# A conditioning sum in two rounded products, and the key tile of the mixing stages in three

## The reference, cut to what matters

```python
for l in range(DEPTH):                      # DEPTH = 2
    x = layer_norm(ALPHA * x + swiglu_half(x, ffn1_w1[l], ffn1_w3[l], ffn1_w2[l]), ...)
    h = x @ w_in[l]                         # 1024 -> 3360 columns
    (a_u, a_v, b_qkv, b_z, b_beta, b_decay, c_q, c_k, c_v, c_r, c_g) = split(h)
    out_b = gated_deltanet(b_qkv, ...)      # conv of 4 taps, silu, q and k normalized per head
    ...
    x = layer_norm(ALPHA * x + concatenate([out_a, out_b, out_c]) @ w_out[l], ...)
    x = layer_norm(ALPHA * x + swiglu_half(x, ffn2_w1[l], ffn2_w3[l], ffn2_w2[l]), ...)
```

## Time and profile before

| | |
|---|---|
| median of 3 runs | 2219.01 us (2215.41 to 2221.36) |
| the profiled execution | 2216.92 us, of which 2215.1 us are the span |
| TensorE busy | 97% of the span |
| VectorE busy | 46% |
| ScalarE busy | 33% |
| GpSimd busy | 4% |
| granted TensorE clock | 1.00 of full speed |
| HBM traffic | 632.39 MB, mean 285 GB/s |

### The profile page before, as it was taken

One profiled execution on the slowest core, in us unless ns is written; L12 is line 12 of the kernel. 1 busy time (PEld: TensorE's weight loads), 2 busy tenths in 40 slices (PEclk: granted clock), 3 DMA queues, 4 the chain that ended last, 5 costly groups with the idle time before them and its releaser, 6 DMA issues. The chain is left out here.

```text
span 2215.1 us, 30365 instructions
## 1 busy us (share of the span) xinstructions
PE 2153.3 (97%) x12435; PEld 1330.2 (60%) x12436; DVE 1025.1 (46%) x1419; ACT 728.0 (33%) x1134; POOL 91.5 (4%) x139
## 2 busy tenths in 40 slices
PE   8999999999999999999999999999999999999998
PEld 7887877888888787788877643333333333333332
DVE  5664776855766568676559741111111111111111
ACT  5433334533543343363436631111111111111111
POOL 5000020000000002000011000000000000000000
PEclk9999999999999999999999999999999999999999
DMA  9762422786487352178636679999999999999998
GB/s 329 232 237 89 156 77 86 246 288 217 134 282 245 120 179 82 41 234 270 218 129 192 261 308 418 429 428 428 428 429 428 429 428 428 428 428 428 428 428 350
DMA packets 192741, 632.39 MB, mean 285 GB/s; under 512 B 31296, under 2 KB 127568, under 8 KB 166272
## 3 DMA queue, kind: packets, MB, share of 16 engines
q1 hardware_dynamic: 192640, 630.93, 73.7%
HBM read 629.82 MB, written 1.07 MB: 285 GB/s over the span
## 5 line engine op out<-in xcount | busy, mean ns | idle before, releaser
L450 PE MATMUL banks<-room_rounded 128*128 128x512 f32 x1824 | 430.4, 391 | 0.0
L450 PEld LDWEIGHTS banks<-room_rounded 128*128 128x128 f32 x1824 | 339.5, 188 | 69.0
L390 DVE TENSOR_TENSOR room_rounded<-memory,room_rounded 128x2048 fp32r<-128x2048 f32 x132 | 299.3, 2292 | 101.4 <-ACT room_rounded L384 96.2
L3351 DVE TENSOR_SCALAR attend_words<-banks 128x512 f32<-128x512 f32 x32 | 22.1, 692 | 557.0 <-PE banks L3087 557.0
L384 ACT CAST room_rounded<-memory 128x2048 fp32r<-128x2048 f32 x132 | 247.8, 1904 | 72.4 <-PE banks L468 63.5
L468 PE MATMUL banks<-room_rounded 128*128 128x512 f32 x1056 | 248.2, 390 | 0.3
L3087 PE MATMUL banks<-memory 128*64 128x512 f32 x1088 | 242.7, 594 | 0.0
L468 PEld LDWEIGHTS banks<-room_rounded 128*128 128x128 f32 x1056 | 197.6, 188 | 42.8 <-DVE room_rounded L637 2.1
L3087 PEld LDWEIGHTS banks<-memory 128*64 128x64 f32 x1088 | 75.1, 136 | 150.8 <-issue 147.7
L3087 PE MATMUL banks<-attend_later,memory 128*64 128x512 f32 x672 | 152.1, 594 | 0.1
L547 ACT ACTIVATE memory<-banks 128x256 f32<-128x256 f32 x88 | 33.8, 384 | 313.0 <-PE banks L450 295.4
(11 more groups left out here) (473 smaller groups left out, 2756.2 us busy)
## 6 DMA issues: line engine op xcount, KB each, us to landing
memory<-in_ffn_w SPq DMA_DIRECT2D x132, 1024.0 KB, 7.4
memory<-in_w_gate_up SPq DMA_DIRECT2D x62, 2048.0 KB, 22.5
attend_later<-in_w_gate_up SPq DMA_DIRECT2D x39, 2048.0 KB, 23.8
memory<-in_w_down SPq DMA_DIRECT2D x25, 2048.0 KB, 24.1
attend_later<-in_w_down SPq DMA_DIRECT2D x19, 2048.0 KB, 23.4
attend_words<-in_w_gate_up SPq DMA_DIRECT2D x17, 2048.0 KB, 22.7
memory<-in_w_in SPq DMA_DIRECT2D x32, 1024.0 KB, 7.1
memory<-in_w_ada SPq DMA_DIRECT2D x32, 768.0 KB, 5.3
```

The costliest lines, as they stand in the source:

```text
L390: nc.vector.tensor_tensor(b, chip.ring[:, chip.slot(base + i), :], a.bitcast(F32), ALU.subtract).then_inc(chip.used, 1)
L450: m = nc.tensor.matmul(psum[:, GU + tt, :], x_parts[:, xp, k, tt * P:tt * P + P], rows, start=(n == 0), stop=(n == 3 * KD - 1))
L3351: ts(room.gate, psum[:, GATE_BANK, :], 7.0, None, ALU.min).then_inc(s["g_ready"], 1)
```

## The change: what it does

Two things are changed. `sum_ada` takes its operand in two rounded parts, so six rounded products stand for three plain ones; ScalarE makes the leading part (`ada_lead`) in the last step of the stage, and VectorE the rest (`ada_low`) ahead of the sums of the norm. In the mixing stages the key tile is in parts as well: two casts on ScalarE ahead of `evac(3)`, two subtractions on VectorE ahead of `finish_x`, and three rounded products on TensorE. To make room for the new leading parts buffers move (`last_lead`, `late`, `x_low`, `lg_rows`). The queries and keys are no longer copied out of PSUM by VectorE: ScalarE squares them from there, `back(1)` goes to banks 2 and 3, and VectorE multiplies by the inverse norms straight from PSUM.

```diff
@@ sum_ada
-        pe.wait_ge(chip.used, base + load_ada(ADA_ROWS - 1) + 1)
+        pe.wait_ge(*s.at("ada_low", 1))
         for i in range(3):
-            nc.tensor.matmul(psum[0:3, MOD_BANK, :], chip.pick[:, 2 - i:5 - i], ada_acc[:, i * 512:i * 512 + 512],
-                             start=(i == 0), stop=(i == 2))
+            for part in (ada_lead, chip.ada_low):
+                nc.tensor.matmul(psum[0:3, MOD_BANK, :], chip.pick[:, 2 - i:5 - i], part[:, i * 512:i * 512 + 512],
+                                 start=(i == 0 and part is ada_lead), stop=(i == 2 and part is chip.ada_low))
@@ ffn_phase, scalar
                 silu(ft, 1)
+                if ft + 1 == STEPS:
+                    act.wait_ge(chip.used, base + load_ada(ADA_ROWS - 1) + 1)
+                    nc.scalar.copy(ada_lead, ada_acc).then_inc(s["ada_lead"], 1)
@@ ffn_phase, vector
+            dve.wait_ge(*s.at("ada_lead", 1))
+            tt_op(chip.ada_low, ada_acc, ada_lead.bitcast(F32), ALU.subtract).then_inc(s["ada_low"], 1)
             norm.sums(dve, 0)
@@ mix_phase
-IN_PARTS = (1, 2)
+IN_PARTS = (1, 2, 3)
...
-                pe.wait_ge(s["low"], 3 + half if t == IN_PARTS[0] else SPLITS)
+                pe.wait_ge(s["low"], 3 + half if t == IN_PARTS[0] else NT + 2 * (t - IN_PARTS[0] + 1))
@@ mix_phase, tensor
-            back(1, 4)
+            back(1, 2)
@@ mix_phase, scalar
             lead(act, 2, 1)
-            for n in range(1, 4):
-                evac(n)
+            evac(1)
+            evac(2)
+            lead(act, 3, 0)
+            lead(act, 3, 1)
+            evac(3)
...
             silu(1)
+            for t, bank in ((0, 4), (1, 2)):
+                for tt in range(NT):
+                    act.wait_ge(s["back"], 2 * t + tt + 1)
+                    func(sq[:, tt, 512 * t:512 * t + 512], psum[:, bank + tt, :], ACT.Square).then_inc(s["squared"], 1)
@@ mix_phase, vector
             take_mod(chip, s)
-            for i in range(2):
-                low(dve, IN_PARTS[1], i, 5 + i)
+            for i in range(4):
+                low(dve, IN_PARTS[1 + i // 2], i % 2, 5 + i)
             finish_x(chip, s, dve, chain)
...
-            take_back(0, 4)
             convolve(1, range(4))
...
-            take_back(1, 4)
-
-            dve.wait_ge(s["tok"], 4)
-            chain(tt_op(sq, qk, qk, ALU.mult))
-            nc.vector.tensor_reduce(ss.rearrange("p (t h) -> p t h", t=NT), sq, AX, ALU.add).then_inc(s["ss"], 1)
+            dve.wait_ge(s["squared"], 2 * NT)
+            nc.vector.tensor_reduce(ss.rearrange("p (t h) -> p t h", t=NT), sq.rearrange("p t (h d) -> p t h d", d=64), AX, ALU.add)\
+                .then_inc(s["ss"], 1)
...
-                chain(tt_op(qk[:, tt, :, :], qk[:, tt, :, :], each_col(rn[:, 16 * tt:16 * tt + 16], 64), ALU.mult))
+                for i, bank in enumerate((4, 2)):
+                    chain(tt_op(qk[:, tt, 8 * i:8 * i + 8, :], heads(bank + tt),
+                                each_col(rn[:, 16 * tt + 8 * i:16 * tt + 8 * i + 8], 64), ALU.mult))
                 scale_first(tt)
```

More of the change, by code:

```diff
@@ L113, in __init__ @@
         self.gbT = w.take(16).rearrange("p (s k) -> p s k", s=2)
-        self.pick = w.take(5)
+        self.pick = self.rounded[:, w.at:w.at + 5]
+        w.take(5)
         self.modT = w.take(24).rearrange("p (s k) -> p s k", s=3)
@@ L119, in __init__ @@
         self.bias_table = self.rounded[:, w.at + D:w.at + 2 * D]
+        odd = w.at % 8
+        self.ada_low = nc.alloc_sbuf_tensor_at("ada_low", [P, ADA_BLOCK + odd], F32R, offset=at + 4 * (w.at - odd))[:, odd:odd + ADA_BLOCK]
         self.norm_gb = w.take(2 * D).rearrange("p (s d) -> p s d", s=2)
@@ L651, in ffn_phase @@
     return Stage(norm, lead, low, emit)
-FFN = "columns acc_zero acc_bias mod_row mod_stored pchain gu0 gu1 x_lead x_low lead hidden hidden_lead hidden_low turned gate down chain " + POST_NORM
+FFN = "columns acc_zero acc_bias ada_lead ada_low mod_row mod_stored pchain gu0 gu1 x_lead x_low lead hidden hidden_lead hidden_low turned gate down chain " + POST_NORM
 def ffn_counts(NT, steps, rows_before, mod_before):
     tiles = sum(what != "ada" for what, *_ in ffn_order(steps))
-    counts = dict(acc_zero=1, acc_bias=16, gu0=steps, gu1=steps, x_lead=NT, x_low=NT, lead=tiles, hidden=NT * steps, hidden_lead=steps,
+    counts = dict(acc_zero=1, acc_bias=16, ada_lead=1, ada_low=1, gu0=steps, gu1=steps, x_lead=NT, x_low=NT, lead=tiles, hidden=NT * steps, hidden_lead=steps,
                   hidden_low=steps, turned=steps, gate=NT * steps, down=steps - 1 + 2 * NT, norm_gbT=32, variance=NT, deviation=NT,
@@ L775, in _ @@
                 nc.gpsimd.memset(chip.eps[:, i:i + 1], v)
-            chain(nc.gpsimd.memset(chip.pick, 0.0))
-            nc.gpsimd.memset(chip.pick[:, 2:3], 1.0)
+            chain(nc.gpsimd.memset(chip.pick.bitcast(F32), 0.0))
+            nc.gpsimd.memset(chip.pick[:, 2:3].bitcast(F32), 1.0)
         @block.sync
@@ L840 @@
        "ub_mm wt_mm ub wt scan_a scan_q u_rows scan_o o_rows scan_s state b_ss b_rms b_out "
-       "mixed_turned mixed_T mixed lead low ") + POST_NORM
+       "mixed_turned mixed_T mixed lead low squared ") + POST_NORM
 def mix_loads(chip, l, w_in, w_out):
@@ L872, in mix_phase @@
     LT, PT = (per_head(region[:, 1024 * i:1024 * i + 1024]) for i in range(2))
-    x_low = rounded("low", w.at, 2048)
     x_first = rounded("x_first", w.at + 2048, 2048)
-    first_leads = rounded("first_leads", w.at + 4096, 8 * MT)
+    x_low = rounded("low", w.at + 4096, 2048)
+    first_leads = rounded("first_leads", w.at + 6144, 8 * MT)
     out_first = rounded("out_first", w.at - 1060, 2048)
@@ L884, in mix_phase @@
     dm = per_head(dm)
-    late = rounded("late", w.at + 1024, 4096)
     out_later = rounded("out_later", w.at, 6144)
@@ L893, in mix_phase @@
     U = per_head(turned_k)
+    late = rounded("late", w.at, 4096)
     levels = w.take(2048)
@@ L901, in mix_phase @@
     WT = scaled_q.rearrange("p (t c g n) -> p t c g n", t=NT, c=2, g=4)
+    last_lead = rounded("last_lead", w.at, 2048)
     qdT = w.take(1024).rearrange("p (t g n) -> p t g n", t=NT, g=4)
@@ L909, in mix_phase @@
     SCt = take3(4, 64)
-    lg_rows = per_head(chip.tmp.rearrange("p t d -> p (t d)")[:, 0:1024])
+    lg_rows = bk
     sgw, sgT = take3(4, P), take3(4, P)
@@ L925, in mix_phase @@
     x_parts = (by_k(x_first), by_k(x_low))
-    lead_rooms = (first_leads[:, 0:4 * MT], first_leads[:, 4 * MT:8 * MT], late[:, 0:2048], late[:, 2048:4096])
+    lead_rooms = (first_leads[:, 0:4 * MT], first_leads[:, 4 * MT:8 * MT], late[:, 0:2048], late[:, 2048:4096],
+                  chip.tmp_rounded, last_lead)
     def tile_parts(t, i):
@@ L946, in mix_phase @@
     end = base + NW + 4
+    sq = chip.tmp
     heads = lambda bank: psum[:, bank, :].rearrange("p (h n) -> p h n", h=8)
@@ L1078, in back @@
                 pe.wait_ge(s["silu"], t + 1)
+                if t == 0:
+                    pe.wait_ge(s["par"], 1)
+                elif t == 1:
+                    pe.wait_ge(s["dm_arg"], 2)
                 for tt in range(NT):
-                    n = 2 * t + tt
-                    if n == 0:
-                        pe.wait_ge(s["par"], 1)
-                    if n >= 2:
-                        pe.wait_ge(s["tok"], n - 1)
                     for c in range(4):
@@ L1161, in turn_heads @@
             def turn_heads(tt):
[L1163 removed]
                 if tt == 0:
[L1165 to L1166 removed]
+                    pe.wait_ge(s["scaled"], 2)
                 else:
@@ L1380, in _ @@
             solution(1)
-            pe.wait_ge(s["tok"], 6)
+            pe.wait_ge(s["tok"], 2)
             scan(0, lambda: unit(12, 0, 4), lambda: unit(12, 4, 8))
@@ L1819, in _ @@
                     take_back(2, 0)
-                    dve.wait_ge(s["tok"], 6)
+                    dve.wait_ge(s["tok"], 2)
                     scale_values(0)
```

5 lines of the change are left out of this document (1 added, 4 removed).

## The result

| | before | after |
|---|---|---|
| median, us | 2217.69 (20 runs beside those of after) | 2222.92 (20 runs, 2218.62 to 2228.57) |
| ratio to before, 95% | | 1.0023 [1.0015, 1.0031] |
| profiled execution: time; span; granted clock | 2216.92; 2215.1; 1.00 | 2221.38; 2219.6; 0.995 |

The change costs 5.2 us (2222.92 - 2217.69): inside the 0.3% called no change, but the 95% interval lies wholly above 1. The predicted time was 2222.3, in a range from 2214 to 2228; the predicted change was +3.3.

A forecast was written before the change was run, and what follows sets the result against it. Ahead of the experts TensorE is hardly ever idle, so shifts there were taken to reach the end whole. First mixing stage +4.7, second +2.5, feed-forward ends -3.9 make +3.3 us on the median 2219.01: 2222.3, range 2214 to 2228.

The forecast's parts named there:

- The conditioning sum, -3.9: Feed-forward ends: six rounded products for three plain ones free 1.3 us at three ends, 0 at the fourth.
- The covers: Feed-forward ends: ScalarE's 1.43 us cast fits a 2.78 us wait, VectorE's 1.72 us subtraction a 1.73 us wait; cost 0.
- the rival on the norm's sums: Feed-forward ends: VectorE's subtraction pushes the norm's sums, up to 6.9 us over four ends, 2229.2; chance 0.06.
- The stands: Mixing stages: TensorE waits at gate_low and for glowT behind key tile splitting; 6.2 us late in the first, 4.0 second.
- The rounded unit, 1.3 each: Key tile on TensorE: a unit in parts takes 5.9 us against 7.20, two units in each mixing stage.
- unit 6 saving nothing: First mixing stage: the decay gates' chain, also 6.2 us late, sets the time, so only unit 7 saves 1.3.
- the loads come in time: Rival, mixing stages: key tile lands early enough, both stages gain 5.6 us together, kernel 9.5, to 2209.5; chance 0.12.
- Queries and keys, -0.2: Mixing stages: TensorE's 1.53 us wait ahead of back(1) shortens by 0 to 1.5 us, taken as 0.2.
- The clock: Rival, mixing stages: granted clock falls in the new 4.1 us stand, making the kernel slower; chance 0.12.
- I am wrong if [...] the granted clock leaves 1.00 there: Sign against the forecast: casts end before TensorE reaches gate_low, or granted clock leaves 1.00 there.
- Behind that TensorE does not wait for VectorE until the level products, so the rest is worth 0: Mixing stages, behind the wait ahead of back(1): VectorE's remaining freed time gains 0.
- 4.7 + 2.5 - 3.9 = +3.3: Sum in us: first mixing stage 6.2 - 1.3 - 0.2, second 4.0 - 1.3 - 0.2, feed-forward ends -3.9.

The follow-up runs named there:

- sum_only: The kernel before with only the conditioning sum in rounded parts; 0.9979 of the kernel before.
- no_sum: The changed kernel with the conditioning sum back in three plain products; 1.0044 of the kernel before.
- late_split: The changed kernel with the key tile's casts moved behind the silu and fifth evac, its subtractions behind glowT; 0.9978 of the kernel before.
- late_rest: The changed kernel with only VectorE's two key tile subtractions moved behind the copy glowT; 1.0015 of the kernel before.
- early_loads: The changed kernel with the key tile's two loads issued earlier on SyncE, engine orders kept; 0.9984 of the kernel before.
- queries_only: The kernel before with only queries and keys normalized from PSUM; 1.0001 of the kernel before.
- the filled stand: The changed kernel with unused products put ahead of TensorE's waits, eight at gate_low and four at gate_up_product; 1.0031 of the kernel before.
- padded2: The change without the key tile in parts, plus 16 small unused float32 products ahead of gate_low in each mixing stage; 1.0042 of the kernel before.
- held_all2: late_split with the second pair of w_out loads held until the last level product; 2209.33 us, 0.9966 of the kernel before.
- plain_keys: The changed kernel without the key tile in parts, its casts and subtractions; 0.9978 of the kernel before.
- plain_held: plain_keys with the second pair of w_out loads held until the last level product; 2209.46 us, 0.9960 of the kernel before.
- held_mid2: late_split with the second pair of w_out loads held until the third level's product; 0.9985 of the kernel before.

## Why the prediction was right, and where it was not

**The conditioning sum, -3.9.** Right. 2.68 to 1.47 us between neighbours' starts at three ends, with 0.17 more at the turn ahead of it; nothing at the fourth. sum_only and no_sum both give 4.6, against 3.9 forecast; the difference is within their intervals. The covers held: neither the cast nor the subtraction pushed anything, and the rival on the norm's sums is out.

**The stands.** Right in place, sequence and cause: 3.76 us (4.1 forecast) ahead of `gate_low`, L1113 5.97 us late (6.2) in the first stage, 2.91 (4.0) in the second. There `gate_low` stood 0.70 us, not 1.9, since the second half's cast began 1 us sooner than the earlier trace rows let one expect. late_split, late_rest and early_loads show each of the two blocks by itself.

**The rounded unit, 1.3 each, and unit 6 saving nothing.** Right: 1.2 to 1.3 in unit 7, 0.2 in unit 6, whose chain then has TensorE wait 0.96. On this rests an error in a rival: "the loads come in time" was priced at 2.8 a stage. With the loads in time a stage gives 0.2 + 1.2 + 0.2 = 1.6, since the decay-gate chain holds unit 6 there too.

**Queries and keys, -0.2.** Right: 37.02 to 36.82 up to the first key product. queries_only: 1.0001.

**The clock.** This is where the prediction's account failed, though its range held. "I am wrong if [...] the granted clock leaves 1.00 there" was its own sign, and the clock did. The prediction gave the fall 0.12, on top of the sum, and counted half of that above 2225.7, which asks for a price of 2225.7 - 2222.3 = 3.4 us or more. No run shows a price of that size. The clock fell in both stages, and cost nothing in the first, where TensorE would have stood for `glowT`, and 2.0 us in unit 6 of the second. That is also why the 2 us ahead of L1113 in the first stage show as 0.44: the 1.6 us that unit 5 took longer filled them. What the runs show of the cause: 0.50 behind 3.76, 2.89 and 1.98 us of idling (after, late_rest, after), no fall behind late_rest's 1.18, and 1.00 in the filled stand. In padded2 the clock fell with TensorE busy (last section).

**What was not in the sum.** "Behind that TensorE does not wait for VectorE until the level products, so the rest is worth 0" looked at waits for engines only. The level products have a wait that no engine ends (1.57 and 1.62 us before) and that moves with the count of instructions (padded2) and goes with the loads (held_all2). With 32 more products ahead of them in the first stage, 64 in the second, it is longer by 0.6 and 0.3 us and the burst by 1.3 and 0.5 in the change. The view of waits had the row all along, as a wait on "issue".

**The whole.** Forecast: 4.7 + 2.5 - 3.9 = +3.3. Found: first stage 5.97 - 0.20 - 1.19 - 0.20 = +4.4, second 2.91 + 1.79 - 1.32 - 0.20 = +3.2, 64x64 products and behind +1.2 and +0.2, the four ends -3.6. That makes +5.3 by the profiles, against +5.2 measured. The sum came within 2 us partly because two misses cancel: a stand 1.1 us shorter in the second stage, and the clock's 2.0 us there. That the time itself, 2222.3, came within 0.6 us of 2222.92 is luck: the change was forecast 1.9 us too small, and it was added to a median of 3 runs (2219.01) that lay 1.3 us above the one of 20.

**Open.** In bursts of the key tile in parts the products also run slower behind the dry wait at a granted clock of 1.00 (after, first stage: 13.33 us for 412 products, 32.4 ns each; plain_keys 11.66 for 380, 30.7; held_all2 29.7). The second stage has it with the plain tile too (before: 12.22 us for 380, 32.2 each). No run shows why. And why the clock fell behind 0.96 us of waiting in held_all2's second stage and not in its first is not settled.

## What to carry to other kernels

The tile in parts needed its data earlier than the plain one, on two engines that took their work in the program's order (in the changed kernel's first stage ScalarE's first cast began at 224.58, TensorE's first product of the tile at 238.54): find the landing before the place of the cast, and put the cast behind everything that others wait for. A saving counts only up to the next chain that is due: one look at what else ends at the unit's end (here the decay gates) settles half of it. Where many small products follow each other, as 64x64 ones every 30 ns here, look for waits that no engine ends (0.9 to 2.6 us here) and try to keep big transfers out of that stretch; the bursts became 1.0 to 3.4 us shorter each. The whole kernels differ by 0.12% and 0.18% (late_split to held_all2, plain_keys to plain_held: 2.7 and 4.0 us); the first difference is inside the noise, the second just outside it.

## What the runs showed of the hardware

- Waits without a releaser in TensorE's bursts of 64x64 products (30 ns each; before, 5.90 us for 195) took 0.9 to 2.6 us in each of 22 bursts with 2 MB in flight and were absent in the 6 bursts without (held_mid2, held_all2, plain_held). Each ended 2.2 to 2.5 us after a 16 KB packet of the instruction queue began, and the place moved with the number of instructions ahead: 32 products more, 31 sooner (before and after, first stage). So they are taken for waits for instructions. The profile counts both queues on the same 16 transfer engines (late_split, 5.7 to 7.7 us into the burst: 55.4% and 3.0%).
- The granted clock dropped to 0.50 for 3.41 us behind dry waits too: in 8 of the 11 bursts with a dry wait of 1.95 to 2.61 us, in none of the 11 with 0.89 to 1.80.
- It also dropped with TensorE busy. In padded2, 32 recorded 128x16 products took 3.64 us (0.11 us each, nearly the 0.119 of a rounded product of 256 columns), TensorE was busy for all 2.00 us from 228 to 230, and the clock was 0.50 in the 2 us behind:

```profile
226.15 3.64 PE L1106 MATMUL banks<-memory 128*128 128x16 f32 x32
```

```profile
228.00:230.00 2.00, 2.00 (x21) 1.98 (x21) 0.00 (x0) 0.00 (x0) 0.00 (x0) 1.00 1.06 389
230.00:232.00 2.00, 2.00 (x12) 2.00 (x11) 0.41 (x1) 0.00 (x0) 0.00 (x0) 0.50 0.75 270
```
